# Block one's attention outputs: values stationary, weights moving, two heads side by side, with inverse sums and gates put on the weights by GpSimd

## What is computed

```python
for l in range(2):
    h = rmsnorm(x, norm_mix[l])
    proj = h @ w_in[l]                                   # 1024 -> 3476
    y_m = mlstm(...)                                     # 4 heads of 128, 512 features
    y_b = moba(b_q, b_k, b_v, ...)                       # 4 heads of 64
    y_n = nsa(n_q, n_kc, n_vc, n_ks, n_vs, n_kw, n_vw, n_g, ...)   # 4 heads of 64
    x = x + concatenate([y_m, y_b, y_n]) @ w_out[l]
    u = square(relu(rmsnorm(x, norm_ffn[l]) @ w_ff1[l]))
    x = x + u @ w_ff2[l]
```

```python
gates = sigmoid(g_pre).reshape(B, S, 3, H)
return g[0] * o_c + g[1] * o_s + g[2] * o_w
```

## Time and profile before

| | |
|---|---|
| median of 3 runs | 1093.7 us (1092.07 to 1094.06) |
| the profiled execution | 1093.48 us |
| its span | 1091.7 us |
| TensorE busy | 1070.7 us, 98% of the span |
| TensorE's weight loads | 913.0 us, 84% |
| VectorE busy | 737.6 us, 68% |
| ScalarE busy | 619.4 us, 57% |
| GpSimd busy | 62.0 us, 6% |
| chain that ended last | 83% TensorE, 7% VectorE, 4% ScalarE |

### The profile page before, as it was taken

One profiled execution on the slowest core, in us unless ns is written; L12 is line 12 of the kernel. 1 busy time (PEld: TensorE's weight loads), 2 busy tenths in 40 slices (PEclk: granted clock), 3 DMA queues, 4 the chain that ended last, 5 costly groups with the idle time before them and its releaser, 6 DMA issues.

```text
span 1091.7 us, 16525 instructions
## 1 busy us (share of the span) xinstructions
PE 1070.7 (98%) x6300; PEld 913.0 (84%) x6300; DVE 737.6 (68%) x1280; ACT 619.4 (57%) x1039; POOL 62.0 (6%) x80
## 2 busy tenths in 40 slices
PE   9999999999999999999999999999999999999997
PEld 7888878888888988888888887898988778989886
DVE  5789777677667888687766675773455756844555
ACT  6776754344436768563444354857556558565562
POOL 1010110000000100110000000004000000040000
PEclk9999999999999999999999999999999999999999
DMA  9853365555657544346566644654444456544441
GB/s 314 270 154 117 97 190 180 190 173 186 210 183 215 169 114 133 123 152 200 170 213 193 193 156 137 211 155 136 118 135 137 132 155 195 154 137 134 136 134 59
DMA packets 89403, 179.03 MB, mean 164 GB/s; under 512 B 8989, under 2 KB 20637, under 8 KB 89325
## 3 DMA queue, kind: packets, MB, share of 16 engines
q1 hardware_dynamic: 88605, 176.58, 52.0%
q10 hardware_dynamic: 720, 1.40, 0.4%
HBM read 176.90 MB, written 1.05 MB: 163 GB/s over the span
## 4 chain that ended last, share of the span: by engine, by line
PE 83%; DVE 7%; ACT 4%; issue 3%; DMA 1%; SPq 1%; DVEq 0%; POOL 0%; POOLq 0%; ACTq 0%
PE bank L830 19%; PE bank L832 18%; PE bank L831 18%; PE bank L896 11%; PE bank L898 5%; DVE w_lo L1767 2%; PE bank L982 2%; PE bank L931 2%; PE bank L1029 1%; ACT w_hi L1368 1%; DMA raw<-in_w_in 1%; PE bank L1039 1%; PE bank L1038 1%; PE bank L1037 1%; PE bank L1292 1%
## 5 line engine op out<-in xcount | busy, mean ns | idle before, releaser
L1767 DVE TENSOR_TENSOR w_lo<-raw,w_hi 128x1024 fp32r<-128x1024 f32 (+1 forms) x319 | 385.4, 1220 | 238.1 <-ACT w_hi L1368 235.3
L1368 ACT ACTIVATE w_hi<-raw 128x1024 fp32r<-128x1024 f32 (+1 forms) x319 | 331.0, 1054 | 182.8 <-PE bank L832 96.6
L830 PE MATMUL bank<-w_hi,h_parts 128*128 128x512 f32 (+1 forms) x448 | 179.9, 402 | 2.9 <-DVE w_lo L1809 1.5
L896 PE MATMUL bank<-h_parts,w_hi 128*128 128x512 f32 x512 | 181.5, 398 | 1.0 <-DVE arena L2131 0.7
L832 PE MATMUL bank<-w_hi,h_parts 128*128 128x512 f32 (+1 forms) x448 | 173.5, 387 | 0.0
L831 PE MATMUL bank<-w_lo,h_parts 128*128 128x512 f32 (+1 forms) x448 | 173.3, 387 | 0.0
L898 PE MATMUL bank<-h_parts,w_lo 128*128 128x256 f32 x512 | 143.6, 280 | 0.0
L896 PEld LDWEIGHTS bank<-h_parts,w_hi 128*128 128x128 f32 x512 | 96.1, 188 | 25.5 <-issue 2.6
L830 PE MATMUL bank<-h_parts,w_hi 128*128 128x256 f32 x384 | 112.3, 292 | 1.0 <-DVE w_lo L1767 1.0
L832 PE MATMUL bank<-h_parts,w_lo 128*128 128x256 f32 x384 | 108.5, 282 | 0.0
L831 PE MATMUL bank<-h_parts,w_hi 128*128 128x256 f32 x384 | 108.5, 282 | 0.0
(11 more groups left out here) (294 smaller groups left out, 1542.7 us busy)
## 6 DMA issues: line engine op xcount, KB each, us to landing
raw<-in_w_in SPq DMA_DIRECT2D x143, 512.0 KB, 3.9
raw<-in_w_ff SPq DMA_DIRECT2D x128, 512.0 KB, 4.3
raw<-in_w_out SPq DMA_DIRECT2D x40, 512.0 KB, 3.3
raw<-in_w_in SPq DMA_DIRECT2D x8, 404.0 KB, 5.4
xn<-in_cmp_w SPq DMA_DIRECT2D x8, 256.0 KB, 5.3
x_sb<-in_x SPq DMA_DIRECT2D x2, 512.0 KB, 9.2
mix<-in_cmp_w SPq DMA_DIRECT2D x4, 256.0 KB, 4.2
gain<-in_cmp_w SPq DMA_DIRECT2D x4, 256.0 KB, 5.6
```

The costliest lines, as they stand in the source:

```text
L830: pe.matmul(out_ap, s_hi, m_hi, start=start, stop=False, **kw)
L896: pe.matmul(ps[:, :].rearrange("p (a t) -> p a t", a=2), hi[:, kk, f], h_parts[:, :, k, :], start=k == 0, stop=False, skip_group_check=True)
L1368: act.activation(slot(w_hi, u), slot(raw, u), ACT.Copy).then_inc(hi_ready, 1)
L1767: dve.tensor_tensor(slot(w_lo, u), slot(raw, u), slot(w_hi, u).bitcast(F32), ALU.subtract)\
```

## The change

The outputs of the twelve heads are formed by feature instead of by token.

- `value_pair` (new, on TensorE) does V for two heads at once: the values of a head (128 tokens by 64 features) are stationary, the turned weights move (256 columns for keys 0 to 127, 128 for keys 128 to 255), and the two heads write partitions 0 to 63 and 64 to 127 of bank 7. It stands where V of the odd head stood. Heads 0 to 3 fill one bank; heads 4 to 11 add up in another, `o_s` and `o_w` of a head in the same place, and the two products of `cmp_o` add to it too, with `vc_diag` stationary.
- So the row's inverse sum and the gate have to be on the weights before they are turned. A new stage N of a pair of heads stands in `heads1` at lag 1, behind E and ahead of S. In it VectorE's `row_inverses` waits for `exp_ready` of the pair's second head and writes three factors for each head (`block_inv`): two instructions for heads 0 to 3, three with gates. GpSimd's `scale_weights` waits for that and multiplies `probs` of both heads in place by them, one instruction of 128x384 each (`weights_scaled`).
- T waits for `weights_scaled` of its head instead of `exp_ready`.
- `epilogue1`, the addition for `cmp_o` and `mix_turn` 2 and 3 with their transposes go. ScalarE and VectorE split the two banks straight into `mixT1_hi[1]` and `mixT1_lo[1]`, behind V of heads 3 and 11.

Nothing else moves; the loads and their order are the same.

```diff
+BY_FEATURE = ("att1",)
...
-            for stage, lag in (("V", 4), ("T", 2), ("E", 1), ("S", 0)):
-                for h in range(12):
+            for stage, lag in (("V", 4), ("T", 2), ("E", 1), ("N", 1), ("S", 0)):
+                for h in range(stage == "V", 12, 2 if stage in ("V", "N") else 1):
...
-                if p == 25:
-                    single(2, "mix_turn", 0, l, 2)
...
-                single(7, "mix_turn", 0, l, 3)
...
+            def value_pair(ps, lo, values_of, weights_of, first):
+
+                for b in range(NT):
+                    for c in range(2):
+                        mm = pe.matmul(ps[HD * c:HD * c + HD, lo + b * P:lo + T], values_of[c](b), weights_of[c][:, b * T:T + b * P],
+                                       start=first and b == 0, stop=b == 1, skip_group_check=True)
+                return mm
...
+                    elif kind in BY_FEATURE:
+                        pe.wait_ge(weights_scaled[kind], len(heads_of(kind, l)) * l + h + 1)
...
-                        ps = open_bank(s)
-                        for i in range(NT):
-                            mm = pe.matmul(ps[:, i * T:(i + 1) * T], p_cmpT[:, i, :],
-                                           vc_diag[:, :, :].rearrange("p h d -> p (h d)"), start=True, stop=True)
-                        close(mm, s)
+                        ps = bank[bank_of["att1", l, "O", 1]]
+                        for c in range(2):
+                            pe.matmul(ps[:, c * T:(c + 1) * T], vc_diag[:, 2 * c:2 * c + 2, :].rearrange("p h d -> p (h d)"),
+                                      p_cmpT[:, :, :].rearrange("p i t -> p (i t)"), start=False, stop=False, skip_group_check=True)
...
+            def scale_weights(kind, l, h):
+
+                pool.wait_ge(inverse_ready[kind], len(heads_of(kind, l)) // 2 * l + h // 2 + 1)
+                for c in range(2):
+                    blocks_of = probs[:, (h + c) % 3, :].rearrange("p (b t) -> p b t", b=3)
+                    pool.tensor_tensor(blocks_of, blocks_of, block_inv[:, h // 2 % 2, c, :].unsqueeze(2).broadcast_to([P, 3, P]),
+                                       ALU.mult).then_inc(weights_scaled[kind], 1)
...
+            def row_inverses(kind, l, h, gate):
+
+                dve.wait_ge(exp_ready, nth_head(kind, l, h + 1))
+                g, r = divmod(h, 4)
+                dst, inv, sums = block_inv[:, h // 2 % 2], row_inv[:, 0:2, :], row_sum[:, g % 2, r:r + 2, :]
+                if gate is None:
+                    link(dve.reciprocal(dst[:, :, 0:2], sums))
+                    dve.reciprocal(dst[:, :, 2:3], sums[:, :, 1:2]).then_inc(inverse_ready[kind], 1)
+                else:
+                    link(dve.reciprocal(inv, sums))
+                    tt(dst[:, :, 0:2], inv, gate, ALU.mult)
+                    dve.tensor_tensor(dst[:, :, 2:3], inv[:, :, 1:2], gate[:, :, 1:2], ALU.mult).then_inc(inverse_ready[kind], 1)
```

More of the change, by code:

```diff
@@ L182, in tail, with columns_of @@
             norm_turn(n, order[2] // 2, order[2] % 2)
+    def columns_of(kind, h):
+        if kind == "att1" and h > 3:
+            return 1, 4, 11
+        return h // 4, h - h % 4, h - h % 4 + 3
     def head_steps(name, h, stage, groups_of):
@@ L191, in head_steps @@
             use((*name, "T", h), 6)
+        elif stage == "V" and name[0] in BY_FEATURE:
+            g, first, last = columns_of(name[0], h)
+            if h == first + 1:
+                use((*name, "O", g), 7)
+            if h == last:
+                done((*name, "O", g))
         elif stage == "V" and name[0] == "diff":
@@ L562, in hybrid_blocks @@
         row_nb = few(4, NT)
+        block_inv = few(2, 2, 3)
         row_sum, row_inv = few(2, 4, NT), few(4, NT)
@@ L1030, in head_stage @@
                     close(mm, (*name, "T", h))
+                elif kind in BY_FEATURE:
+                    g, first, last = columns_of(kind, h)
+                    for c in range(2):
+                        drained(pe, (*name, "T", h - 1 + c))
+                    ps = open_bank((*name, "O", g)) if h == first + 1 else bank[bank_of[(*name, "O", g)]]
+                    mm = value_pair(ps, h // 2 % 2 * T, [heads_of(kind, l)[h - 1 + c][3] for c in range(2)],
+                                    [probsT[:, (h - 1 + c) % 3, :] for c in range(2)], h == first + 1)
+                    if h == last:
+                        close(mm, (*name, "O", g))
                 else:
@@ L1558, in _ @@
                         softmax_stage(kind, l, s[2], s[3])
+                        if s[2] == "V" and s[3] in (3, 11):
+                            g = s[3] // 8
+                            turned(("att1", l, "O", g), mixT1_hi[1][:, 2 * g:2 * g + 2, :])
                     elif kind == "mix_turn":
```

50 lines of the change are left out of this document (18 added, 32 removed).

## The result

The changed kernel takes 1115.97 us (median of 4 runs, 1113.48 to 1118.07) where the kernel before, beside it, takes 1093.85 (4 runs, 1092.07 to 1094.06): a ratio of 1.0205, 95% interval 1.0187 to 1.0223, or 22 us slower. The direction is that of the forecast, and so is the chain in front of the transposes; 1107 and the upper end of 1113 are not: the loss is 22 us, not 13. The profiled execution took 1116.48 with a span of 1114.7; before, the span was 1091.7.

The account below looks back on a forecast made before the run. TensorE was taken as the bound, VectorE right behind. About two thirds of the way from the first walk (7.4 us) to the second (16.4) gave 13.3 us on the median of 1093.7: 1107, range 1099 to 1113.

Parts of the forecast that it names:

- TensorE's saving: TensorE's work in both layers: 14.6 us of values go, 10.2 of value pairs come, 1.4 of mix transposes go; 5.8 less.
- rival (d): Value pairs on TensorE: the array's halves do not run together, 0.65 us more a pair, 2.6 more in all, 1110; chance 0.04.
- The chain in front of T: Transposes of even heads wait for GpSimd's product behind N on VectorE, 6 to 11 us in each layer; chance 0.85.
- Rival (a): Waits in front of T are hidden because VectorE runs earlier; only TensorE's 5.8 us count, 1088; chance 0.07.
- N's price: N's small instructions on VectorE: 0.61 us for a pair with gates, 0.43 without.
- The clock: New TensorE gaps of 2 to 3 us might lower its granted clock, "slower still"; no size or chance given.
- the two walks: Lateness through the pairs: first, nothing else disturbed, 3.7 us a layer; second, GpSimd and VectorE hindering each other, 8.2.
- The exponentials are no limit: ScalarE's exponentials ahead of N: the last of pair 6 ends at 91.6, its sum 0.19 later, 2.5 us before VectorE arrives.
- VectorE never waits again: From pair 6's scores, there at 90.2 with VectorE busy until 91.1, VectorE never waits and its lateness only adds up.
- The wait at `hid`: TensorE's wait of 1.0 us at L2037, behind pair 2, absorbs that much lateness; both layers taken to show the same pattern.
- Interference of GpSimd and VectorE: Each GpSimd product costs VectorE an estimated 0.6 us beside instructions with two SBUF operands; GpSimd loses 0.4 to 1.1.
- table of arrival times: Six pairs in the trace before: when VectorE reaches N's place and TensorE starts T; VectorE up to 1.1 us late for four.

Follow-up runs that it names:

- e1: The changed kernel without N and GpSimd's products, weights undivided, T waiting for the exponentials alone: 1088.35 us, ratio 0.9950 to the kernel before.
- e3: The changed kernel with 26, 26 and 14 products of constants on TensorE ahead of T's wait in pairs 2, 4 and 8: 1109.60 us, ratio 1.0141.
- e15: The changed kernel with ScalarE's exponentials of a pair ahead of its copy of the previous pair's odd transposes: 1110.98 us, ratio 1.0162.
- e2: The changed kernel with GpSimd's products on a spare buffer, T waiting for the exponentials alone, weights undivided: 1103.77 us, ratio 1.0087.
- e5: e1 plus N on VectorE, nothing waiting for it, still without GpSimd's products: 1093.10 us, ratio 0.9996.
- e4: The changed kernel with transposes one projection step later, value pairs of heads 8 to 11 too, and a fourth weights buffer: 1099.83 us, ratio 1.0051.
- e12: The changed kernel with N on GpSimd and the products on ScalarE, transposes in the changed kernel's place, three weights buffers: 1114.26 us, ratio 1.0188.
- e8: e4 with N on GpSimd too, products staying on GpSimd: 1093.20 us, ratio 1.0005.
- e14: The changed kernel with N on GpSimd as well as the products, transposes in the changed kernel's place, three weights buffers: 1118.62 us, ratio 1.0238.
- e6: e4 with both products of each pair on VectorE behind N, none on GpSimd: 1105.21 us, ratio 1.0105.

## Why the prediction was right, and where it was wrong

**TensorE's saving, 5.8 us: right.** e1 measured 5.5. The value pair takes 0.80 from its start to the next T's (78.35 to 79.15) where 0.85 was put down, so rival (d) falls. (The prediction's list of signs says 0.65 for it, which leaves out the 0.2 of its own sum.)

**The chain in front of T, and that it ends slower than before: right.** T of the even heads waits for GpSimd's product, odd heads do not. Rival (a) falls: e1 shows what it would have given, and the change is 28 us above it. N's price (0.57 with gates in pair 8, for 0.61) and the product's (1.97 for two beside taps; 0.95 and 0.08 had been put down for one) hold.

**The clock, named and put at nothing: this is the step that took the time out of the range.** The text said that gaps of 2 to 3 us might lower the granted clock and "that would be slower still", and gave it neither a size nor a chance. e3 holds the clock up and leaves the chain as it is: 1.0141, 15.4 us over the kernel before, where the forecast has 13.3 and the range ends at 19. T of pairs 4, 8 and 10 in e3:

```profile
89.48 0.55 PE L1054 MATMUL bank<-const,probs 128*128 128x128 f32 x3 [0.22 <-POOL probs L1704]
...
109.84 0.55 PE L1054 MATMUL bank<-const,probs 128*128 128x128 f32 x3 [0.24 <-POOL probs L1704]
...
120.06 0.52 PE L1054 MATMUL bank<-const,probs 128*128 128x128 f32 x3 [1.02 <-POOL probs L1704]
```

That is 5.5, 8.2 and 8.8 us late; two thirds of the way between the two walks, as the forecast takes it, makes 6.0, 7.7 and 7.5. In the change itself they are 7.1, 10.3 and 12.3 late. So with the clock up the walks miss by no more than 1.3 us in a layer, and the clock, 9.5 us in the windows and 7 by e3, is the largest term that the sum lacks. With it the 13.3 of the forecast would have been 20 to 23, with the measured 22 among them. No row of before shows what a wait of 3 us does to the clock, since TensorE never stood there for more than 1.5 us. That is a reason for a wider range and for a rival with a chance of its own, not for nothing.

**"The exponentials are no limit": wrong, the second and smaller error.** It was read from pair 6 alone, where they end 1.6 us before T, and compared with VectorE, not with T. For pair 8 they end 0.4 us before T already in the kernel before, behind a copy that waits for TensorE itself. There the lateness is not handed on from VectorE but made anew, in a loop: odd transposes, ScalarE's copy, exponentials, N, product, T, 5.07 us from one T to the next with 3.3 us of TensorE's own work in it. e15 took this part out and 5 us went, the clock behind pair 8 among them. The 1.3 us by which pair 10 is later in e3 than in the forecast fit this loop, but no run parts them from the rest.

**"VectorE never waits again": wrong with it.** It waits at N for ScalarE, 0.5, 0.9 and 1.4 us in pairs 6, 8 and 10 of the first layer. In both walks it only ever got later; in the first TensorE's own work was the longer way by pair 10 (4.5 late, no wait). In the trace T is 12.3 late at pair 10, and waits 0.9 us.

**The wait at `hid`: absorbed once, counted twice.** The walks take 1.0 us off in each layer for it, on the ground that both layers show the same pattern. The list of waits of the kernel before has it once (1.0, 1), in the first layer; this makes the forecast 1 us too low.

**Interference of GpSimd and VectorE: right in kind, about right in size.** Two thirds of a 4.5 us difference between the walks, 3 us in each layer, were forecast; e2 against e5 shows 5 in each layer, about half of it clock; VectorE's instructions themselves are 4.1 us longer there. That it costs as much with nobody waiting for the product, I had not seen when I wrote e2's expectation.

**What was not asked** is the question that e4 answers with one number: whether T could stand a step later. The table of arrival times in the prediction showed VectorE and T within 1.1 us of each other for five pairs, with a step of 3 us to be had.

## What to carry to other kernels

Work put between a producer and its consumer must be set against the distance between their places, not against the load of the engine that gets it: here the same work, shared out among the engines in three ways, brought the kernel 21 to 26 us above the one before at one place and 0 to 6 us above it one step later. The order inside an engine counts beside it (18 us with the exponentials first, at the old place). Work out the room for every repetition (the exponentials had 1.6 us at one pair and 0.4 at the next) and look for loops in which the waiting engine's own output stands ahead of its input in some queue. And a wait on TensorE can have a second price behind it, in the granted clock: here 7 to 9.5 us beside 19.3 us of waits, behind most waits of 1.8 to 3.2 us.

## What the runs showed of the hardware

- The granted clock fell behind TensorE waits of 1.8 to 3.2 us (to 0.56 to 0.69 over the next 3 to 5.5 us), not always at once: behind the 3.17 us wait of pair 4 the transposes and scores still took 0.55 and 0.93 us, and the projection after them 4.45 instead of 2.95. In e12 a wait of 2.26 us left the clock as it was and one of 1.74 did not. Filling the waits with products of constants kept it at 1.00 in both layers.
- GpSimd's product of 128x384 with a factor for each block takes 0.83 us with nothing beside it (e8), 1.0 beside the taps and up to 1.8 where it meets a w_lo.
- A power of -1 of four elements for each partition takes GpSimd 1.0 us (1.01 in e14, 1.0 to 1.9 in e8), a product of the same size 0.2 (in e8 up to 1.3). VectorE's reciprocal takes 0.18.
- VectorE's copies of 128x384 from PSUM are as long beside GpSimd's products as without them (0.56 in e2, 0.55 to 0.56 in e5); copies of 128x128 from SBUF to SBUF are not: 0.44 and 0.39 in e2, 0.23 in e5.
- A GpSimd product costs VectorE about 0.3 us on its other instructions (4.1 us for twelve in e2), where VectorE takes 0.51 to 0.55 to do that product itself (e6).
